# Moving layer 1's split activations to other byte offsets inside the tiles that both layers share

## The reference, cut to what matters

```
for l in range(DEPTH):                       # DEPTH = 2
    xn  = rmsnorm(h, norm1_g[l]) * (1 + sc1) + sh1
    ...                                      # the context stream likewise, in full only in layer 0
    h = h + g1 * token_mix(xn @ w_in[l], k_c, v_c, lp, cos, sin)
    h = h + g2 * sq_relu_mlp(rmsnorm(h, norm2_g[l]) * (1 + sc2) + sh2, w_ff1[l], w_ff2[l])

def token_mix(...):                          # three branches and their gates
    a  = pool_mixer(...) @ lp['pool_out']
    b  = hyena_mixer(...) @ lp['hy_out']
    cm = o.reshape(b_, L, MLA_HEADS * V_HEAD) @ lp['w_o']
    return (ga * a + gb * b + gc * cm) @ lp['w_out']

def sq_relu_mlp(x, w1, w2):
    return jnp.square(jax.nn.relu(x @ w1)) @ w2
```

## Time and profile before

| | before |
|---|---|
| median of 3 runs | 1434.92 us (1434.4 to 1435.6) |
| the profiled execution, its own time | 1434.04 us |
| its span, first to last instruction | 1431.9 us |
| TensorE (PE) matmuls busy | 1389.0 us, 97% of the span |
| weight loads (PEld) busy | 1129.9 us, 79% |
| VectorE (DVE), ScalarE (ACT), GpSimd (POOL) busy | 53%, 38%, 14% |

### The profile page before, as it was taken

How to read it: one execution, slowest core, us unless ns; L and a number is a source line. 1 busy time by engine, 2 the same in 40 slices (tenths; PEclk the granted TensorE clock), 3 DMA queues, 4 the chain that set the end, 5 groups by cost and what they waited for, 6 DMA issues and landing times.

```text
span 1431.9 us, 19716 instructions
## 1 busy us (share of the span) xinstructions
PE 1389.0 (97%) x8132; PEld 1129.9 (79%) x8132; DVE 762.5 (53%) x1091; ACT 545.0 (38%) x843; POOL 199.1 (14%) x185
## 2 busy tenths in 40 slices
PE   8999999999999999999999999989999999999997
PEld 3557756777777887777778888868769989899997
DVE  5455665234443475744223443374866767775664
ACT  5633363232231232533112431243465435553552
POOL 1151000512001144000000002200005212300012
PEclk9999999999999999999999999989999999999999
DMA  9332302444631255234443225422415746555552
GB/s 374 116 136 88 118 16 103 159 157 147 232 136 44 74 199 202 86 145 152 149 167 114 97 92 218 145 83 89 138 38 197 263 136 211 175 189 191 181 190 72
DMA packets 55769, 208.43 MB, mean 146 GB/s; under 512 B 6293, under 2 KB 6677, under 8 KB 54144
## 3 DMA queue, kind: packets, MB, share of 16 engines
q1 hardware_dynamic: 52992, 194.22, 38.2%
q0 software_dynamic: 2688, 12.95, 2.4%
HBM read 203.48 MB, written 3.67 MB: 145 GB/s over the span
## 4 chain that ended last, share of the span: by engine, by line
PE 90%; DVE 4%; ACT 3%; issue 1%; DMA 1%; SPq 0%; POOL 0%; DVEq 0%; ACTq 0%
PE ps L1490 26%; PE ps L1491 25%; PE ps L1492 25%; PE ps L1790 2%; PE ps L1519 2%; PE ps L1888 1%; PE ps L1898 1%; PE ps L1637 1%; PE ps L1801 1%; PE ps L1814 1%; DMA pairs<-in_pairs 1%; DVE rstd L1060 1%; DVE wl L1022 1%; DVE k_t L1258 1%; PE ps L1746 1%
## 5 line engine op out<-in xcount | busy, mean ns | idle before, releaser
L1022 DVE TENSOR_TENSOR wl<-raw,wh 128x1024 fp32r<-128x1024 f32 (+2 forms) x272 | 357.9, 1318 | 235.9 <-ACT wh L716 232.9
L1490 PE MATMUL ps<-xh,wh 128*128 128x512 f32 (+2 forms) x1392 | 474.4, 341 | 3.1 <-DVE xl L1089 1.4
L1491 PE MATMUL ps<-xl,wh 128*128 128x512 f32 (+2 forms) x1392 | 467.9, 336 | 0.0
L1492 PE MATMUL ps<-xh,wl 128*128 128x512 f32 (+2 forms) x1392 | 467.4, 336 | 0.0
L716 ACT ACTIVATE wh<-raw 128x1024 fp32r<-128x1024 f32 (+2 forms) x272 | 283.6, 1043 | 317.9 <-PE ps L1492 317.0
L1490 PEld LDWEIGHTS ps<-xh,wh 128*128 128x128 f32 (+1 forms) x1392 | 262.5, 189 | 43.5 <-issue 10.8
L1492 PEld LDWEIGHTS ps<-xh,wl 128*128 128x128 f32 (+1 forms) x1392 | 263.5, 189 | 29.1
L1491 PEld LDWEIGHTS ps<-xl,wh 128*128 128x128 f32 (+1 forms) x1392 | 262.5, 189 | 28.0 <-issue 1.0
L1490 PE MATMUL ps<-hid_h,wh 128*128 128x512 f32 (+1 forms) x512 | 172.7, 337 | 0.0
L1491 PE MATMUL ps<-hid_l,wh 128*128 128x512 f32 (+1 forms) x512 | 171.9, 336 | 0.0
L1492 PE MATMUL ps<-hid_h,wl 128*128 128x512 f32 (+1 forms) x512 | 171.7, 335 | 0.0
(11 more groups left out here) (237 smaller groups left out, 1437.1 us busy)
## 6 DMA issues: line engine op xcount, KB each, us to landing
raw<-in_units SPq DMA_DIRECT2D x262, 512.0 KB, 3.3
mod_ring<-in_mod_units SPq DMA_DIRECT2D x49, 512.0 KB, 4.0
gap_hy<-in_mod_units SPq DMA_DIRECT2D x15, 512.0 KB, 4.5
pairs<-in_pairs SPq DMA_DIRECT2D x6, 1024.0 KB, 15.2
gap_relu<-in_mod_units SPq DMA_DIRECT2D x7, 512.0 KB, 4.5
filters<-filt POOLq DMA_DIRECT2D x10, 256.0 KB, 2.8
filt<-filters POOLq DMA_DIRECT2D x2, 1280.0 KB, 10.4
ftab<-in_fwd POOLq DMA_DIRECT2D x3, 768.0 KB, 5.0
```

The costliest lines, as they stand in the source:

```text
L1022: dve.tensor_tensor(wl[:, g % SLOTS, 0:n], raw[:, g % SLOTS, 0:n], wh[:, g % SLOTS, 0:n].bitcast(F), ALU.subtract)\
L1490: pe.matmul(dst, w_h, m_h, start=first, stop=False)
L1491: pe.matmul(dst, w_h, m_l, start=False, stop=False)
L1492: return pe.matmul(dst, w_l, m_h, start=False, stop=last)
```

## The change

The named constant goes, and each pair of tiles gets a layer-1 shift of its own: 24 floats (96 bytes) for the tokens, 32 floats (128 bytes) for the branches, 16 floats (64 bytes) for the MLP units. High and low part are shifted alike. Layer 0 stays at 0.

```diff
-SHIFT = 48
 ROOM = 64
...
-        xh_of = by_layer(ctx, "xh", KB, (0, SHIFT))
-        xl_of = by_layer(ctx, "xl", KB, (0, SHIFT))
+        xh_of = by_layer(ctx, "xh", KB, (0, 24))
+        xl_of = by_layer(ctx, "xl", KB, (0, 24))
...
-            fh_of = by_layer(s, "fh", 4, (0, SHIFT))
-            fl_of = by_layer(s, "fl", 4, (0, SHIFT))
+            fh_of = by_layer(s, "fh", 4, (0, 32))
+            fl_of = by_layer(s, "fl", 4, (0, 32))
...
-            hid_h_of = by_layer(s, "hid_h", 16, (0, SHIFT))
-            hid_l_of = by_layer(s, "hid_l", 16, (0, SHIFT))
+            hid_h_of = by_layer(s, "hid_h", 16, (0, 16))
+            hid_l_of = by_layer(s, "hid_l", 16, (0, 16))
```

## The result

The changed kernel takes 1440.39 us, the median of 6 runs (1439.8 to 1444.32), the kernel before 1435.26 us (1433.3 to 1436.08, also 6 runs) measured beside it. The ratio is 1.0047, 95% interval 1.0033 to 1.006: about 5 us slower, where 1428.4 was forecast. The number lies inside the range given, 1424 to 1441 us, but the kernel moved the other way.

A forecast was written before the change was run, and what follows sets the result against it. TensorE's matmul pitch was taken to bound the kernel; the profiled 1434.04 us less 6.5 for the last stretch gave 1427.5, and 0.9 up to the median made 1428.4 us, range 1424 to 1441 us.

The forecast's parts named there:

- The bound: Layer 1's long streams: the end moves with TensorE's pitch alone; matmuls are busy for 97% of the span.
- The two levels: Gapless layer-1 stretches at full clock: pitch 113.3 or 117.8 ns per 256-token matmul, 4.5 ns apart.
- the last stretch: Layer 1, 1250 to 1420 us: 1448 matmuls at the high level, forecast to fall to the low one, 6.5 us.
- all at 120.0: +9.3 us: Layer-1 tokens, 2088 matmuls: the case that all rise to 120.0 ns, +9.3 us.
- the split of 1070 low and 960 high: Layer-1 tokens: estimate of how many matmuls stood at the low and high levels before the change.
- the branches' 0: Layer-1 branches, 288 matmuls, 192 to 128 bytes: taken as 0, bounds -1.1 to +1.3 us.
- the MLP units' forecast -3.5: Layer-1 MLP units, 768 matmuls, 192 to 64 bytes: fall from 117.8 to 113.3 ns, -3.5 us.
- rival 3: Layer 1: all new offsets as bad as shift 0, +11.8 us, 1446.7 us; chance 0.12.
- The lower bound of 111.7: Layer 1's 256-token matmuls: spacing in ns of weight loads alone; a lower pitch would need a faster load.
- Rival 1: Layer 1: nothing happens, restarts behind stalls set the levels, not the offset; 1434.9 us; chance 0.25.
- Rival 2: Layer 1: high level everywhere, as 96 bytes isn't whole 64-byte pieces; +5.0 us, 1439.9 us; chance 0.19.

The follow-up runs named there:

- experiment 11: Kernel before, with a small float32 matmul added ahead of every fourth unit in layer 1's MLP, 16 in all: 1435.0 us against 1437.59.
- experiment 12: Kernel before, with 14 small float32 matmuls added in layer 1's w_out and MLP, most in ff1a: median 1431.02 us against 1434.40, ratio 0.9982.
- experiment 13: Changed kernel (96, 128, 64 bytes), with 20 small float32 matmuls added that break layer 1's streams in w_out and the MLP: 1441.69 us, one run.
- experiment 1: Changed kernel, with branches and MLP units put back to 192 bytes and tokens left at 96: 1440.28 us, ratio 1.0029.
- experiment 6: Changed kernel, with branches and MLP units at 192 bytes and 32 bytes of padding ahead of the weights: 1446.97 us, one run.

## Why the prediction was wrong

- **The bound** was right: the end moved with TensorE's pitch, writers and queues stayed as they were.
- **The two levels** 113.3 and 117.8, and 120.0 at offset 0, were read rightly, and so was what a level is worth: 4.5 ns. Experiments 11 to 13 show that a break in the stream can select between the two.
- **The step that failed** is this one: "If a new offset keeps two levels like those at 192 and each stretch lands anew, the last stretch decides, and it stands on the bad side now." The tokens' new offset does not keep them. It has 120.0 alone (experiments 1 and 13). And where the condition held, for the MLP units at 64, the stretch did not land on the other side by itself. It took a break (experiment 13). So the last stretch did not fall by 6.5 us: its MLP units stayed at 117.8, and its tokens rose to 120.0.
- **The terms.** Tokens "all at 120.0: +9.3 us" measured +8.6 (the split of 1070 low and 960 high was off; by the mean pitch of 115.7 some 47% were low); the branches' 0 measured +0.8, inside its bounds; the MLP units' forecast -3.5 measured 0. The tokens' part of rival 3 is what came, and I had given rival 3 a chance of 0.12. I took the mix of levels seen at 192 as what a new offset would bring, although the trace had a second offset, 0, with a single level, and `cqh` was the only row for it at this width. An unknown bounded by 111.7 and 120.0 from a mean of 115.7 has as much room up as down, and the token tiles hold two thirds of the matmuls. The lower bound of 111.7 came from float32 loads of another tile behind one-column matmuls; no 256-token stream went below 113.3.
- **Rival 1** is half true: restarts select the level, but only among those that the distance allows. **Rival 2**'s number, 1439.9, is near the median of 1440.39 by luck: it wanted the tokens at 117.8, and they ran at 120.0. Its reason, 96 not being a multiple of 64, does not carry: 32 bytes at 116.7 is better than 128 at 118.7.
- **The Trainium skill**, page "SBUF — State Buffer", section "SBUF: two separate sides", gives lines of 16 bytes and an independent port for the weight loads, by which all offsets would be alike. The runs disagree: multiples of 16 bytes differ by up to 6.7 ns per matmul, and the partner is the weight tile (experiment 6). That TensorE would wait on another engine is not what 120.0 against 113.3 shows, though the prediction set the two against each other. Why two reads of one engine cost each other time, and why this distance and no other, no run here shows.

## What to carry to other kernels

In a stream of float32r matmuls with a 128-column weight load each, look at the distance of start times, not at durations or busy shares: 113.3, 117.8 and 120.0 ns all read as a PE that is 100% busy. The byte distance between moving operand and weight block is a tuning knob of up to 6% of the pitch at 256 tokens (3% at 512); it must be measured for each width of the moving operand, and here tiles that share a distance share its levels. Where a distance has two levels, compare profiles of several executions before believing a difference. A cheap break in the stream can be worth more than a new offset: here 14 of them gave 3.4 us net, and the new offsets lost 5.

## What the runs showed of the hardware that was not expected

- The same program, data and addresses run at two steady pitches, 113.3 and 117.8 ns. The high one was kept for over 1400 matmuls, the low one for 384 without a break (experiment 1).
- Five of the eleven distances show two levels, each with a pair of its own: 113.3 and 117.8 at 64 and 192, 117.3 and 118.7 at 160, 116.7 and 119.2 at 208, 116.7 and 117.8 at 32.
- The good distance depends on the width: 192 bytes gives 113.3 or 117.8 against 120.0 at 256 tokens, and 233.4 against 227.1 at 512.
- After the same stalls, the time at 1.2 GHz varies between executions, of the kernel before too: 13 to 16 matmuls of the 256-token form in seven profiles, 41 to 44 in seven, 29 and 36 in the other two, worth up to some 2.9 us.
